# The norm in mid-layer in two halves of the tokens

## The chip, the core and the metric

The kernel runs on one core of a Trainium2 chip. The metric is the device time in microseconds of one execution; lower is better. A core has five engines that run side by side, each in its own order, and meet at semaphores: TensorE (PE, matmuls, with the weight loads shown apart as PEld), VectorE (DVE), ScalarE (ACT), GpSimd (POOL) and SyncE (SP). The last two issue DMAs here.

## What is computed

A trunk of two layers over 512 tokens of width 1024, all in float32. Each layer has two residual steps:

```python
h = modulate(rms_norm(x, norm1_g[l]), sh1, sc1)
z = h @ w_in[l]
# conformer convolution, short gated convolution and differential attention on parts of z
x = x + g1[:, None, :] * mix          # mix = concat(ya, yb, yc) @ w_out[l]
h = modulate(rms_norm(x, norm2_g[l]), sh2, sc2)
x = x + g2[:, None, :] * swiglu(h, w_gate_up[l], w_down[l])
# rms_norm(x, g) = x * rsqrt(mean(x * x, -1) + 1e-6) * g
# modulate(h, shift, scale) = h * (1 + scale) + shift
```

The second norm of a layer, between the projection `w_out` and the gate/up product, is the one that the change touches. It is a norm over the 1024 features of each token, so the tokens are independent of each other.

## The kernel before

**Layout.** Features lie on partitions, tokens in columns: `xT` is 128 partitions x 8 chunks x 512 tokens. Each product is made from two parts of either side: `h_hi` and `h_lo`, `w_hi` and `w_lo` (FP32R), with three matmuls per 128x128 block (hi x hi, lo x hi, hi x lo; `product`, L1308). TensorE writes a result of 128 features x 512 tokens into one of the eight PSUM banks.

**Units.** The weights come as a stream of units of 128x1024, in the order in which TensorE uses them. A unit is loaded by SP into one of two `raw` buffers, ScalarE copies it to `w_hi` (`split_hi`, L547), and VectorE subtracts to get `w_lo` (`split_lo`, L852). For units 12 to 33 of layer 0 (`lo_by_dma`, L60) ScalarE writes the negative copy as well, and POOL issues a DMA that adds the raw weights to it (`add_raw`, L435). Four units fit in the ring, so unit u + 4 is split when unit u is done: that is `step(u)` (L554) on ScalarE. SP's next load into a raw buffer waits for the split of the unit in it. A unit is 8 blocks, 24 matmuls (`unit`, L1323).

**The projection.** Eight units, U_OUT to U_OUT+7, give the eight chunks of `mix`. After each, VectorE adds it to `xT` (`add_to_x`, L1100), ScalarE squares the new chunk (`square_x`, L560), VectorE sums the squares (`norm_sum`, L1091). Chunk 7's square is not summed by VectorE.

**The norm.** `norm_stat` (L1384, called in L1573) makes two FP32 matmuls with a matrix of ones, of the sum of seven squares and of the square of chunk 7; each is two instructions in the profile. ScalarE takes Ln and Exp of that (`norm_rstd`, L568, called in L821); ahead of it, in ScalarE's order, stands `step(U + U_OUT + 7)` (L820), which splits unit U_GU+3. Then the eight chunks of h are made: VectorE scales a chunk by gain and rstd into one of two buffers (`norm_apply`, L927), ScalarE adds the shift and writes `h_hi` (`norm_hi`, L584), VectorE writes `h_lo` (`norm_lo`, L936). VectorE's order is scaling 0, scaling 1, difference 0, scaling 2, difference 1 and so on (`norm`, L944); a scaling from the third on waits until the difference two chunks before, the instruction ahead of it, has ended.

**Gate/up.** The first two units, U_GU and U_GU+1, go chunk by chunk into banks 0 and 1, as the chunks of h arrive (`units_by_chunk`, L1331, called in L1575): four matmuls per chunk after `h_hi`, two more after `h_lo`. The third and the fourth unit follow whole, and then the other 40 in a loop.

All orders are written out by hand; there is no scheduler. ScalarE's around the norm:

```python
for s in range(N_OUT):
    if s < N_OUT - 1:
        step(U + U_OUT + s)
    square_x(2 * l + 1, s)
step(U + U_OUT + N_OUT - 1)
norm_rstd(2 * l + 1)
```

## Time and profile before

| | us |
|---|---|
| runs (3): median, lowest, highest | 1224.09, 1223.81, 1224.74 |
| the profiled execution | 1223.83 |
| its span in the profile | 1222.0 |
| TensorE busy in the span | 1185.0 (97%) |
| VectorE busy | 709.3 (58%) |
| ScalarE busy | 487.2 (40%) |
| mean granted clock of TensorE | 0.989 of full |

The span is the time from the first to the last instruction of one execution, the device time is a little longer. A busy time is the time in which at least one instruction of the engine was in flight. Matmuls are pipelined, so one of 0.39 us is followed by the next after less than that; their spacing is read from the starts. "[idle before <-releaser]" behind an instruction is the time that its engine stood still before it, and what ended that. The granted clock is a share of TensorE's full clock of 2.4 GHz; its other level, 0.50, is 1.2 GHz.

### The profile page before, as it was taken

The numbers are of one execution on the slowest core, as the hardware profiler recorded it, in microseconds if no ns is written. First come the engines' busy times: TensorE is split into PE (matmuls) and PEld (weight loads), VectorE is DVE, ScalarE is ACT, GpSimd is POOL, SyncE is SP. The second block draws the span as 40 slices with busy tenths as digits, with TensorE's granted clock in tenths as the row PEclk, the third lists the DMA queues.
The fourth block names the chain that finished last, engine by engine and source line by source line (L and its number), as shares of the span: only waits on it lengthen the run. The fifth ranks groups of instructions, "written<-read, shape, count | busy, mean of one in ns | idle before, by whom it ended". The sixth has DMA issues, their size and how long they took to land.

```text
span 1222.0 us, 14230 instructions
## 1 busy us (share of the span) xinstructions
PE 1185.0 (97%) x5102; PEld 928.4 (76%) x5102; DVE 709.3 (58%) x1014; ACT 487.2 (40%) x728; POOL 111.7 (9%) x185
## 2 busy tenths in 40 slices
PE   8999999789999999999989999999999999999998
PEld 6887545668888888888868875467788888888887
DVE  7888987766556433466656999746633333333331
ACT  5556787552322322322242356774432232322220
POOL 2411322211012000111000001000000000000000
PEclk9999999889999999999989999999999999999999
DMA  8787455976565222677413321103223223233322
GB/s 306 249 232 161 95 111 203 297 207 224 189 198 185 97 103 88 261 253 246 148 56 104 100 71 52 52 1 121 78 94 103 86 103 102 87 103 104 104 103 86
DMA packets 47498, 169.92 MB, mean 139 GB/s; under 512 B 5537, under 2 KB 5665, under 8 KB 47458
## 3 DMA queue, kind: packets, MB, share of 16 engines
q1 hardware_dynamic: 30386, 107.13, 25.9%
q0 software_dynamic: 17072, 62.27, 17.1%
q8 instruction: 23, 0.38, 0.1%
q14 instruction: 17, 0.14, 0.0%
HBM read 167.28 MB, written 2.10 MB: 139 GB/s over the span
## 4 chain that ended last, share of the span: by engine, by line
PE 80%; DVE 11%; ACT 5%; issue 3%; DMA 1%; POOL 0%; DVEq 0%; ACTq 0%
PE ps L1311 22%; PE ps L1313 21%; PE ps L1312 21%; PE ps L1341 3%; DVE uc L974 3%; ACT prob L632 2%; PE ps L1525 1%; PE ps L1345 1%; DVE w_lo L857 1%; PE ps L1357 1%; PE ps L1358 1%; PE ps L1362 1%; DVE neg_max L1055 1%; PE ps L1372 1%; PE ps L1374 1%
## 5 line engine op out<-in xcount | busy, mean ns | idle before, releaser
L550 ACT ACTIVATE w_hi<-raw 128x1024 fp32r<-128x1024 f32 x196 | 207.7, 1060 | 574.6 <-PE ps L1313 492.9
L857 DVE TENSOR_TENSOR w_lo<-raw,w_hi 128x1024 fp32r<-128x1024 f32 x174 | 213.4, 1227 | 266.5 <-ACT w_hi L550 266.3
L1311 PE MATMUL ps<-h_hi,w_hi 128*128 128x512 f32 x848 | 335.9, 396 | 7.0 <-DMA w_lo<-w_stream 7.0
L1313 PE MATMUL ps<-h_lo,w_hi 128*128 128x512 f32 x848 | 331.3, 391 | 0.0
L1312 PE MATMUL ps<-h_hi,w_lo 128*128 128x512 f32 x848 | 331.2, 391 | 0.0
L1311 PEld LDWEIGHTS ps<-h_hi,w_hi 128*128 128x128 f32 x848 | 159.9, 189 | 56.0 <-issue 16.7
L1313 PEld LDWEIGHTS ps<-h_lo,w_hi 128*128 128x128 f32 x848 | 159.8, 188 | 33.9
L1312 PEld LDWEIGHTS ps<-h_hi,w_lo 128*128 128x128 f32 x848 | 160.0, 189 | 31.7
L1311 PE MATMUL ps<-gu_hi,w_hi 128*128 128x512 f32 x352 | 136.9, 389 | 0.0
L1312 PE MATMUL ps<-gu_hi,w_lo 128*128 128x512 f32 x352 | 136.9, 389 | 0.0
L1313 PE MATMUL ps<-gu_lo,w_hi 128*128 128x512 f32 x352 | 136.9, 389 | 0.0
L1259 DVE TENSOR_TENSOR work_b<-ps,work_a 128x512 f32<-128x512 f32 x44 | 30.4, 692 | 115.5 <-PE ps L1313 92.1
L974 DVE SCALAR_TENSOR_TENSOR uc<-ua,pcol,uc 128x512 f32<-128x512 f32 x120 | 83.6, 743 | 0.0
L1312 PEld LDWEIGHTS ps<-gu_hi,w_lo 128*128 128x128 f32 x352 | 66.1, 188 | 13.8
L1311 PEld LDWEIGHTS ps<-gu_hi,w_hi 128*128 128x128 f32 x352 | 66.1, 188 | 13.7
L1313 PEld LDWEIGHTS ps<-gu_lo,w_hi 128*128 128x128 f32 x352 | 66.1, 188 | 13.7
L1372 PE MATMUL ps<-w_hi,h_hi 128*128 128x512 f32 x192 | 75.0, 391 | 1.1 <-DVE w_lo L857 1.1
L1374 PE MATMUL ps<-w_hi,h_lo 128*128 128x512 f32 x192 | 74.7, 389 | 0.0
L1373 PE MATMUL ps<-w_lo,h_hi 128*128 128x512 f32 x192 | 74.7, 389 | 0.0
L632 ACT ACTIVATE prob<-ps,neg_max 128x512 f32<-128x512 f32 x64 | 43.3, 683 | 33.6 <-DVE neg_max L1055 33.6
L1104 DVE SCALAR_TENSOR_TENSOR xT<-ps,mod,xT 128x512 f32<-128x512 f32 x32 | 24.0, 750 | 56.1 <-PE ps L1313 53.6
L444 POOL TENSOR_SCALAR row_mix<-row_inv,neg_lam 128x1 f32<-128x1 f32 x32 | 25.7, 803 | 219.7 <-DVE row_inv L1062 219.7
(171 smaller groups left out, 1312.8 us busy)
## 6 DMA issues: line engine op xcount, KB each, us to landing
raw<-w_stream SPq DMA_DIRECT2D x196, 512.0 KB, 3.3
ada_ring_gu<-ada POOLq DMA_DIRECT2D x28, 512.0 KB, 4.2
ada_ring_late<-ada POOLq DMA_DIRECT2D x28, 512.0 KB, 4.9
w_lo<-w_stream POOLq DMA_DIRECT2D x22, 512.0 KB, 8.1
ada_ring_first<-ada POOLq DMA_DIRECT2D x16, 512.0 KB, 5.7
ada_ring_mid_a<-ada POOLq DMA_DIRECT2D x12, 512.0 KB, 5.5
ada_ring_mid_b<-ada POOLq DMA_DIRECT2D x12, 512.0 KB, 5.4
xT<-x_t SPq DMA_DIRECT2D x4, 512.0 KB, 5.7
```

The source lines that it names most:

```text
L550: act.activation(w_hi[:, u % RING, :], raw[:, u % RAW, :], ACT.Copy).then_inc(s_whi, 1)
L632: act.activation(prob[:, it % PROBS, comp, :], ps[:, 2 * (it % 2) + comp, :], ACT.Exp, bias=neg_max[:, it, comp:comp + 1], accum_out=row_s ...
L857: dve.tensor_tensor(w_lo[:, u % RING, :], raw[:, u % RAW, :], w_hi[:, u % RING, :].bitcast(F32), ALU.subtract).then_inc(s_wlo, 1)
L974: dve.scalar_tensor_tensor(uc[:, c, :], ua[:, c, j:j + T], w, uc[:, c, :], ALU.mult, ALU.add).then_inc(s_tap, 1)
L1259: dve.tensor_tensor(wb[:, f, :], ps[:, j, :], wa[:, f, :], ALU.mult).then_inc(s_pr, 1)
L1311: pe.matmul(dst, whi, rhs[0][:, n, :], start=start, stop=False)
L1312: pe.matmul(dst, wlo, rhs[0][:, n, :], start=False, stop=False)
L1313: return pe.matmul(dst, whi, rhs[1][:, n, :], start=False, stop=stop)
L1341: pe.matmul(ps[:, bank, :], wp[:, u % RING, n * P:(n + 1) * P], h_hi[:, n, :], start=b == 0 and wp is w_hi, stop=False)
L1372: pe.matmul(ps[:, bank, :], hs[0], ws[0], start=n == 0, stop=False)
L1373: pe.matmul(ps[:, bank, :], hs[0], ws[1], start=False, stop=False)
L1374: return pe.matmul(ps[:, bank, :], hs[1], ws[0], start=False, stop=n == KC - 1)
```

## The change

In each layer the stretch from the last projection unit to the first two gate/up units is done in two halves of the tokens, columns 0 to 255 and 256 to 511:

- The last unit writes its first half into bank 6 and its second into bank 2, one after the other, in 48 matmuls of 256 columns. Amid the second half (after four blocks) the statistic of the first half is taken.
- VectorE adds each half to chunk 7 of `xT`, ScalarE squares it. In layer 0 the second gain (`make_gain`) is made ahead of these additions instead of after.
- Ln and Exp are taken of each half; those of the second half stand in ScalarE's order behind `h_hi` of chunk 2 of the first half.
- VectorE goes through the eight chunks for the first half, then for the second.
- TensorE's first two gate/up units go through the eight chunks for the first half, then for the second, with the second half's statistic after two chunks of the first. A chunk's six matmuls wait for `h_lo`, so for both parts.
- The split of unit U_GU+3 moves: on ScalarE from ahead of the norm's Ln to between the two halves of `h_hi`, in layer 1 on VectorE from ahead of the scaling to behind chunk 1 of the second half.

The diff, without the new semaphores and blank lines:

```diff
+HALVES = (slice(0, T // 2), slice(T // 2, T))
...
+        B_LAST, B_HALF_STAT = (6, 2), (7, 4)
...
+            def square_half(l, half):
+                act.wait_ge(s_xnew if half else s_xhalf, KC * (2 * l + 1) if half else l + 1)
+                act.wait_ge(s_sum, (KC - 1) * 2 * l + KC - 2)
+                c = HALVES[half]
+                act.activation(wa[:, 1, c], xT[:, KC - 1, c], ACT.Square).then_inc(s_sq if half else s_sqhalf, 1)
+            def rstd_half(l, half):
+                n = 2 * l + 1
+                c = HALVES[half]
+                if half:
+                    act.wait_ge(s_nstat, n + 1)
+                    act.activation(rstd[:, 0, c], ps[:, B_HALF_STAT[half], c], ACT.Ln, scale=1.0 / D,
+                                   bias=eps[:]).then_inc(s_nln, 1)
+                    act.wait_ge(s_nln, n + 1)
+                    act.activation(rstd[:, 0, c], rstd[:, 0, c], ACT.Exp, scale=-0.5).then_inc(s_nrs, 1)
+                else:
+                    act.wait_ge(s_sthalf, l + 1)
+                    act.activation(rstd[:, 0, c], ps[:, B_HALF_STAT[half], c], ACT.Ln, scale=1.0 / D,
+                                   bias=eps[:]).then_inc(s_lnhalf, 1)
+                    act.wait_ge(s_lnhalf, l + 1)
+                    act.activation(rstd[:, 0, c], rstd[:, 0, c], ACT.Exp, scale=-0.5).then_inc(s_rshalf, 1)
+            def hi_half(l, half, k):
+                n = 2 * l + 1
+                c = HALVES[half]
+                if half:
+                    act.wait_ge(s_t, KC * n + k + 1)
+                else:
+                    act.wait_ge(s_thalf, KC * l + k + 1)
+                a = mod_at(SH2, k)
+                act.activation(h_hi[:, k, c], wb[:, k % 2, c], ACT.Identity,
+                               bias=mod[:, l, a:a + 1]).then_inc(s_hhi if half else s_hihalf, 1)
...
                 for s in range(N_OUT):
                     if s < N_OUT - 1:
                         step(U + U_OUT + s)
-                    square_x(2 * l + 1, s)
-                step(U + U_OUT + N_OUT - 1)
-                norm_rstd(2 * l + 1)
+                        square_x(2 * l + 1, s)
+                square_half(l, 0)
+                rstd_half(l, 0)
+                square_half(l, 1)
                 act.wait_ge(s_gain, 2 * l + 1)
                 for k in range(KC):
-                    norm_hi(l, 1, k)
+                    hi_half(l, 0, k)
+                    if k == 2:
+                        rstd_half(l, 1)
+                step(U + U_OUT + N_OUT - 1)
+                for k in range(KC):
...
+            def norm_halves(l):
+                n = 2 * l + 1
+                dve.wait_ge(s_gain, n)
+                for half in range(2):
+                    c = HALVES[half]
+                    if half:
+                        dve.wait_ge(s_nrs, n + 1)
+                    else:
+                        dve.wait_ge(s_rshalf, l + 1)
+                    for k in range(KC + 1):
+                        if k < KC:
+                            if k >= 2 and half:
+                                dve.wait_ge(s_h, KC * n + k - 1)
+                            elif k >= 2:
+                                dve.wait_ge(s_hhalf, KC * l + k - 1)
+                            dve.scalar_tensor_tensor(wb[:, k % 2, c], xT[:, k, c], gain[:, l, 1, k:k + 1],
+                                                     rstd[:, 0, c], ALU.mult,
+                                                     ALU.mult).then_inc(s_t if half else s_thalf, 1)
+                        if k:
+                            a = mod_at(SH2, k - 1)
+                            if half:
+                                dve.wait_ge(s_hhi, KC * n + k)
+                            else:
+                                dve.wait_ge(s_hihalf, KC * l + k)
+                            dve.scalar_tensor_tensor(h_lo[:, k - 1, c], wb[:, (k - 1) % 2, c], mod[:, l, a:a + 1],
+                                                     h_hi[:, k - 1, c].bitcast(F32), ALU.add,
+                                                     ALU.subtract).then_inc(s_h if half else s_hhalf, 1)
+                        if half and k == 2:
+                            split_lo(UNITS * l + U_GU + RING - 1)
...
+            def add_last_to_x(l, unit):
+                a = mod_at(G1, KC - 1)
+                for half in range(2):
+                    c = HALVES[half]
+                    if half:
+                        dve.wait_ge(s_unit, unit)
+                    else:
+                        dve.wait_ge(s_uhalf, l + 1)
+                    dve.scalar_tensor_tensor(xT[:, KC - 1, c], ps[:, B_LAST[half], c], mod[:, l, a:a + 1],
+                                             xT[:, KC - 1, c], ALU.mult,
+                                             ALU.add).then_inc(s_xnew if half else s_xhalf, 1)
...
-                    add_to_x(l, s, B_OUT[s], G1, U + U_OUT + s + 1)
-                    split_lo(U + U_OUT + s + RING)
+                    if s < N_OUT - 1:
+                        add_to_x(l, s, B_OUT[s], G1, U + U_OUT + s + 1)
+                    else:
+                        if l == 0:
+                            make_gain(0, 1)
+                        add_last_to_x(l, U + U_OUT + s + 1)
+                    if s < N_OUT - 1:
+                        split_lo(U + U_OUT + s + RING)
                     if s < N_OUT - 1:
                         norm_sum(2 * l + 1, s)
                     if l == 0 and s < N_OUT - 2:
                         for m in range(M_MID + 12 + 2 * s - (s == 0), M_MID + 14 + 2 * s):
                             mod_dot(m)
-                if l == 0:
-                    make_gain(0, 1)
-                norm(l, 1)
+                norm_halves(l)
...
+            def stat_half(l, half):
+                n = 2 * l + 1
+                c = HALVES[half]
+                pe.wait_ge(s_sum, (KC - 1) * n)
+                pe.matmul(ps[:, B_HALF_STAT[half], c], ones[:], sq_sum[:, c], start=True, stop=False)
+                if half:
+                    pe.wait_ge(s_sq, KC * (n + 1))
+                else:
+                    pe.wait_ge(s_sqhalf, l + 1)
+                pe.matmul(ps[:, B_HALF_STAT[half], c], ones[:], wa[:, 1, c], start=False,
+                          stop=True).then_inc(s_nstat if half else s_sthalf, 1)
+            def product_half(bank, w, b, half, start, stop):
+                c = HALVES[half]
+                whi, wlo = w_hi[:, w, b * P:(b + 1) * P], w_lo[:, w, b * P:(b + 1) * P]
+                pe.matmul(ps[:, bank, c], whi, h_hi[:, b, c], start=start, stop=False)
+                pe.matmul(ps[:, bank, c], wlo, h_hi[:, b, c], start=False, stop=False)
+                return pe.matmul(ps[:, bank, c], whi, h_lo[:, b, c], start=False, stop=stop)
+            def last_unit(l, u):
+                weights_split(u)
+                for half in range(2):
+                    if half:
+                        pe.wait_ge(s_xnew, 2 * KC * l + 4)
+                    for b in range(KC):
+                        if half and b == KC // 2:
+                            stat_half(l, 0)
+                        mm = product_half(B_LAST[half], u % RING, b, half, b == 0, b == KC - 1)
+                    mm.then_inc(s_unit if half else s_uhalf, 1)
+            def first_units(l, us):
+                n = 2 * l + 1
+                for u in us:
+                    weights_split(u)
+                for half in range(2):
+                    for b in range(KC):
+                        if half:
+                            pe.wait_ge(s_h, KC * n + b + 1)
+                        else:
+                            pe.wait_ge(s_hhalf, KC * l + b + 1)
+                        for bank, u in enumerate(us):
+                            mm = product_half(bank, u % RING, b, half, b == 0, b == KC - 1)
+                            if half and b == KC - 1:
+                                mm.then_inc(s_unit, 1)
+                        if not half and b == 1:
+                            stat_half(l, 1)
...
-                    unit(U + U_OUT + s, B_OUT[s], h, order)
-                norm_stat(2 * l + 1)
-
-                units_by_chunk([U + U_GU, U + U_GU + 1], (0, 1), order, s_hhi, s_h, KC * (2 * l + 1))
+                    if s < N_OUT - 1:
+                        unit(U + U_OUT + s, B_OUT[s], h, order)
+                    else:
+                        last_unit(l, U + U_OUT + s)
+                first_units(l, [U + U_GU, U + U_GU + 1])
```

## Rows read from the trace of the kernel before

**Rows 1.** The page: busy time by engine; the chain that ended last, by engine
```profile
PE 1185.0 (97%) x5102; PEld 928.4 (76%) x5102; DVE 709.3 (58%) x1014; ACT 487.2 (40%) x728; POOL 111.7 (9%) x185
...
PE 80%; DVE 11%; ACT 5%; issue 3%; DMA 1%; POOL 0%; DVEq 0%; ACTq 0%
```

**Rows 2.** TensorE's timeline, layer 0: start us, us, engine, line, operation, count, [idle before]
```profile
252.70 1.02 PE L1387 MATMUL ps<-sq_sum,ones 128*128 128x512 f32 x2
...
254.45 1.12 PE L1389 MATMUL ps<-work_a,ones 128*128 128x512 f32 x2 [0.73 <-ACT work_a L566]
...
259.27 0.76 PE L1341 MATMUL ps<-h_hi,w_hi 128*128 128x512 f32 x1 [3.69 <-ACT h_hi L588]
...
272.70 0.39 PE L1311 MATMUL ps<-h_hi,w_hi 128*128 128x512 f32 x1
...
278.14 0.39 PE L1311 MATMUL ps<-h_hi,w_hi 128*128 128x512 f32 x1
```

**Rows 3.** TensorE's timeline, layer 1
```profile
851.91 1.02 PE L1387 MATMUL ps<-sq_sum,ones 128*128 128x512 f32 x2
...
857.83 0.47 PE L1341 MATMUL ps<-h_hi,w_hi 128*128 128x512 f32 x1 [3.13 <-ACT h_hi L588]
...
870.47 0.39 PE L1311 MATMUL ps<-h_hi,w_hi 128*128 128x512 f32 x1
```

**Rows 4.** Stretches: length, busy us of PE, PEld, DVE, ACT, POOL, granted clock, DMA, GB/s
```profile
257.00:259.00 2.00, 0.00 (x0) 0.00 (x0) 1.42 (x2) 1.12 (x2) 0.47 (x1) 0.65 1.04 225
264.00:265.00 1.00, 1.00 (x5) 0.75 (x5) 0.96 (x3) 0.35 (x1) 0.00 (x0) 0.78 0.09 16
858.00:859.00 1.00, 1.00 (x4) 0.82 (x4) 0.96 (x2) 0.30 (x1) 0.00 (x0) 0.68 0.58 234
```

**Rows 5.** VectorE's timeline, layer 0
```profile
250.63 0.15 DVE L916 TENSOR_TENSOR mod<-mod_raw,pcol 128x3 f32<-128x3 f32 x1
...
257.55 1.42 DVE L933 SCALAR_TENSOR_TENSOR work_b<-xT,gain,rstd 128x512 f32<-128x512 f32 x2 [3.75 <-ACT rstd L572]
...
259.16 0.75 DVE L941 SCALAR_TENSOR_TENSOR h_lo<-work_b,mod,h_hi 128x512 fp32r<-128x512 f32 x1 [0.19 <-ACT h_hi L588]
...
259.94 0.75 DVE L933 SCALAR_TENSOR_TENSOR work_b<-xT,gain,rstd 128x512 f32<-128x512 f32 x1
...
260.61 0.75 DVE L941 SCALAR_TENSOR_TENSOR h_lo<-work_b,mod,h_hi 128x512 fp32r<-128x512 f32 x1
```

**Rows 6.** ScalarE's timeline, layer 0
```profile
255.25 1.04 ACT L552 ACTIVATE w_lo<-raw 128x1024 fp32r<-128x1024 f32 x1
...
256.19 0.67 ACT L570 ACTIVATE rstd<-ps,eps 128x512 f32<-128x512 f32 x1
...
256.89 0.63 ACT L572 ACTIVATE rstd<-rstd 128x512 f32<-128x512 f32 x1
...
260.73 0.72 ACT L588 ACTIVATE h_hi<-work_b,mod 128x512 fp32r<-128x512 f32 x1 [0.99 <-DVE work_b L933]
```

**Rows 7.** Groups of VectorE and ScalarE by form: count, busy us, mean ns, idle before
```profile
L857 DVE TENSOR_TENSOR w_lo<-raw,w_hi 128x1024 fp32r<-128x1024 f32 x174 | 213.4, 1227 | 266.5 <-ACT w_hi L550 266.3
...
L1046 DVE TENSOR_TENSOR tb<-tn,tabs 128x256 f32<-128x256 f32 x32 | 12.1, 418 | 0.0
...
L1041 DVE TENSOR_TENSOR ta<-tn,tabs 128x512 f32<-128x512 f32 x16 | 11.1, 692 | 0.6
...
L550 ACT ACTIVATE w_hi<-raw 128x1024 fp32r<-128x1024 f32 x196 | 207.7, 1060 | 574.6 <-PE ps L1313 492.9 <-PE ps L1374 49.3 <-DMA raw<-w_stream 15.1
...
L566 ACT ACTIVATE work_a<-xT 128x512 f32<-128x512 f32 x24 | 14.9, 620 | 18.6 <-DVE xT L1104 18.5
```

**Rows 8.** TensorE's timeline, keys' transposes in layer 0
```profile
105.26 1.91 PE L1458 MATMUL ps<-ident,qk 128*128 128x128 f32 x16
```

**Rows 9.** The page's DMA issues: count, KB each, median us to landing
```profile
raw<-w_stream SPq DMA_DIRECT2D x196, 512.0 KB, 3.3
...
w_lo<-w_stream POOLq DMA_DIRECT2D x22, 512.0 KB, 8.1
```

More of the change, by code:

```diff
@@ L325, in encoder_kernel @@
         s_h = sem("h_ready")
+        s_uhalf = sem("first_half_unit_done")
+        s_xhalf = sem("first_half_x_updated")
+        s_sqhalf = sem("first_half_x_squared")
+        s_sthalf = sem("first_half_norm_stat")
+        s_lnhalf = sem("first_half_norm_ln")
+        s_rshalf = sem("first_half_norm_rstd")
+        s_thalf = sem("first_half_norm_scaled")
+        s_hihalf = sem("first_half_h_hi_ready")
+        s_hhalf = sem("first_half_h_ready")
         s_sig = sem("gate_sigmoid")
@@ L818, in _ @@
                         step(U + U_OUT + s)
-                    square_x(2 * l + 1, s)
-                step(U + U_OUT + N_OUT - 1)
-                norm_rstd(2 * l + 1)
+                        square_x(2 * l + 1, s)
+                square_half(l, 0)
+                rstd_half(l, 0)
+                square_half(l, 1)
                 act.wait_ge(s_gain, 2 * l + 1)
                 for k in range(KC):
-                    norm_hi(l, 1, k)
+                    hi_half(l, 0, k)
[3 more added lines that the diff above has]
+                for k in range(KC):
+                    hi_half(l, 1, k)
                 act.preload_act_table_set("silu_and_others")
```

## Prediction

> **What bounds the kernel now.** I read the chain of waits first: TensorE carries 80% of what ends last [rows 1], so only a stretch where TensorE stands still, or runs slowly, can pay. The norm in mid-layer is one, once in each of the two layers. TensorE's timeline shows it. In layer 0 the last unit of the projection has been issued at 252.70 us and the third gate/up unit starts at 272.70: 20.00 us for two sums of squares and two units [rows 2]. In layer 1 it is 851.91 to 870.47, 18.56 us [rows 3]. A unit is 24 matmuls in 278.14 - 272.70 = 5.44 us, 0.227 each [rows 2], so two cost 10.88; the rest, 9.1 and 7.7 us, is the norm. In it TensorE's work is four FP32 instructions of some 0.43, 1.7 us. What is left is waiting (TensorE stands 3.69 us in layer 0 and 3.13 in layer 1 before the first gate/up matmul [rows 2, 3]) and a lower clock. The stretches show the granted clock at 0.65 in 257 to 259 us, on its way from the 2.4 to the 1.2 GHz level after TensorE had been idle since 255.6; it is back within 264 to 265, and in layer 1 it falls in 858 to 859 [rows 4].
>
> The last view is VectorE's. Once the statistic is there, a chunk of h costs a scaling (L933) and a difference (L941): 0.67 from scaling to difference, 0.78 back, where VectorE waits for its own difference to have ended [rows 5]. That is 1.45 us per chunk, against 6 x 0.227 = 1.36 for TensorE. So the two are nearly even, and the change must be priced on both.
>
> **The change, step by step.** Times from here on count from the first matmul of the last unit, 5.44 us before the stretch above: 247.26 us in layer 0, 846.47 in layer 1. In the kernel before, the third gate/up unit starts at 25.44 (layer 0) and 24.00 (layer 1). All stages behind it move with it, as TensorE has no other long wait in a layer's second half; so its new start is the whole effect.
>
> *Prices of a half.* A VectorE operation on 256 columns takes 418 ns, on 512 692 [rows 7]: 0.274 less. The scaling and the difference take 0.75 and follow each other by 0.67 [rows 5]; halves: 0.48 and 0.40, or 0.52 where the next waits for the end. A half chunk is then 0.92, two 1.84 instead of 1.45. ScalarE: 1060 ns for 1024 columns, 620 for 512 [rows 7], so 0.22 less: h_hi 0.50, square 0.40, Ln 0.46, Exp 0.41 [rows 6]. TensorE on 256 columns with these weights is not in the trace. From below it is half of 0.227, 0.113; at 2.4 GHz 512 columns are 0.213, which leaves 0.013 fixed and gives 0.107 + 0.013 = 0.120; from above it is the weight load's own 0.18 (928.4 us in 5102 [rows 1]), if that no longer hides. I take 0.120, because sixteen FP32 transposes of 128 columns, each with its own load, pass in 1.91 us, 0.12 each at most [rows 8], so a load needs no more.
>
> *Last unit.* First half 24 x 0.120 = 2.88; its sum can be added at 3.1, but VectorE is still with the sixth square, mod and gain (250.63 plus two short operations, 3.7 here [rows 5]). Addition and square of chunk 7 end at 4.7. TensorE meanwhile has done four blocks of the second half (4.32) and the first FP32 sum (4.75); so the make_gain moved ahead (0.15) is hidden. The statistic ends at 5.2, the second half at 6.6. Ln and Exp are ready at 6.3, hidden by the second addition, for which VectorE waits until 6.8. The first scaling starts at 7.2 against 257.55 - 247.26 = 10.29 before [rows 5]: **3.1 us earlier**. h_hi and h_lo follow, TensorE begins at 8.9 instead of 12.0 (layer 1: 11.4).
>
> *First half of h.* VectorE delivers a half chunk every 0.92 us, TensorE uses 6 x 0.120 = 0.72. After two chunks (10.5) comes the other half's statistic, 0.85, to 11.4. On ScalarE Ln and Exp of it stand behind h_hi of chunk 2 and ahead of h_hi of chunk 3, and ScalarE is in order: it waits from 9.9 to 11.6, spends 0.9, and h_hi of chunk 3, which could have begun at 10.4, begins at 12.4. Behind it wait VectorE's h_lo, then TensorE. **A new stall of 1.9 us**: h_lo of chunk 3 ends at 13.4, of chunk 7 at 16.9; TensorE ends the half at 17.7.
>
> *Second half of h, layer 0.* ScalarE has first to do the moved split of unit U_GU+3: two copies of 0.94 each [rows 6]. Its h_hi starts at 18.1, h_lo of chunk 0 ends at 19.2, of chunk 7 at 19.2 + 6 x 0.92 + 0.7 = 25.4. TensorE's last block ends at 26.2. **Layer 0: 26.2 - 25.4 = 0.8 us later.** The split's add-DMA waits on POOL for the negative copy: some 18.1, plus 8.1 to land [rows 9], is 26.2, and U_GU+3 is wanted at 26.2 + 5.4 = 31.7, so a unit covers it. SP's next raw load waits for the same copy and needs 3.3 [rows 9], landing long before ScalarE takes it after 26. Without that cover each microsecond late would be one of TensorE's. Behind POOL's add stand loads that wait for products of the gate/up stage, later anyway.
>
> *Layer 1.* One copy on ScalarE, so h_lo of chunk 0 ends at 18.3; but VectorE does the moved w_lo behind chunk 1, 1.14 (1227 ns, less 0.08 of overlap) [rows 7]. Chunk 7 ends at 25.5, TensorE at 26.4. **Layer 1: 26.4 - 24.0 = 2.4 us later.**
>
> *Sum:* +0.8 + 2.4 = +3.2 us. The 3 us gained at the start go to 16 half chunks at 0.92 where 8 whole ones cost 1.45 (3.1 us per layer), and the two stalls come on top; what TensorE got back from the lower clock was never on VectorE's path. The 72 additional matmuls per layer (0.013 each, 0.9) lie mostly in TensorE's new waits. With 0.113 per half matmul, and 0.02 less for each hand-over, the sum is +2.1; with 0.125 and 0.03 more, +4.5. Against the profiled execution, 1223.83 (span 1222.0; 0.26 below the median of the runs, 1224.09), that is 1227.0. About 0.2%, 2.4 us, is what a measurement of this kernel can tell from no change.
>
> A rule on the waits: before, VectorE's next scaling starts 0.78 after a difference whose end it waits for, and a difference starts 0.67 after a scaling whose end it doesn't [rows 5], so that wait costs 0.11. The Trainium skill's page "VectorE: DVE Perf Modes", section "The DRAIN you can't avoid", says that a semaphore between chained operations costs nothing extra. By the row the sum is +3.2; by the rule each half chunk would be 0.81 and the sum +1.1. The row decides.
>
> **Rivals.** *A, not slower:* the fixed part of VectorE's halves does not come twice, and the half scaling and difference follow by 0.335. Then a half chunk is 0.74, TensorE's 0.72 keeps step, and the layers come out at -1.5 and +0.1: 1222.5. For it: no scalar_tensor_tensor of 256 columns is in the trace, and the first scaling does start 3 us earlier. Against: 418 ns and not 346 for the two-tensor form [rows 7]. It decides from about 0.35 us downwards; with both stalls gone too it would be about 1220.
>
> *B, the clock falls in the new gaps:* TensorE stands from 6.6 to 8.9, 12.1 to 13.5 and 17.7 to 19.3 (18.4 in layer 1), and works 0.72 of every 0.92 between. Before, it fell some 2 us into the gap of layer 0 [rows 2, 4], so 2.3 could be enough. At 1.2 GHz a chunk's six half matmuls take up to 1.44, more than 0.92, and the statistic 1.7. A fall at 9 to 10 costs some 1.6 per layer, one late in the second half up to 2.4: 1228.6 in one layer, 1230.2 in both. Against: in layer 1 the whole gap of 3.13 us passed at the full clock, which fell only in 858 to 859 [rows 3, 4].
>
> *C, half matmuls bound by the weight load:* at 0.18 each a chunk takes 1.09, and the layers come out at +6.1 and +7.4: 1237.3. Against: [rows 8], and 0.227 for 512 columns, which leaves no room for a load in series. The Trainium skill, "TensorE: Matmul & The Clock Gate", section "Measured speedup vs the span model", has a load overlap only matmuls of other rows of the array; that would put loads in series here. By that rule C's price or more would hold; the trace disagrees, with 0.227 per pair.
>
> **Chances.** Forecast 0.50, A 0.20, B 0.22, C 0.08. Of the forecast 0.15 falls within 0.2% (+2.1 to +2.4, and what the steps leave uncertain), of A 0.12, the rest of A is faster; B and C are slower. So faster 0.08, same 0.27, slower 0.65. The range leaves out C, A's lower end and B's upper: 1223.0 to 1231.0.
>
> **What the next profile would show.** First scaling 3 us earlier after the last unit began; a step of about 0.92 between half chunks; an idle ScalarE of 1.7 us ahead of the second Ln; h_hi of chunk 3 some 2 us behind chunk 2's successor on VectorE; TensorE's waits split into many of 0.2 us and three of 1.4 to 2.3; the third gate/up unit 26 us behind the last unit's start in both layers. A step of 0.8 or less, or a missing ScalarE stall, would make the prediction wrong to the fast side; half matmuls 0.15 or more apart, or a granted clock of 0.5 in the stretch, to the slow side.

## The result, and the profile after

The kernel with the change took 1228.57 us (median of 6 runs, 1227.85 to 1230.05), the kernel before 1224.74 beside it (6 runs): a ratio of 1.0034, 95% interval 1.0022 to 1.0045. It is slower by some 4 us. The profiled execution of after took 1228.17 us (span 1226.4), that of before 1223.83 (span 1222.0): 4.4 us more in the span.

The page's busy times and the chain of waits, to be held against [rows 1]:

```profile
PE 1188.1 (97%) x5254; PEld 936.0 (76%) x5254; DVE 715.4 (58%) x1048; ACT 493.0 (40%) x750; POOL 112.7 (9%) x185
...
PE 78%; DVE 11%; ACT 5%; issue 3%; DMA 2%; SPq 0%; POOL 0%; DVEq 0%; ACTq 0%
```

VectorE and ScalarE are 6 us busier each, with 34 and 22 instructions more, which is the fixed part of their halves; on the page alone nothing else can be told. The time shows in TensorE's timeline. The first row of each layer below is the first matmul of the last unit, the last one the third gate/up unit [rows 2, 3]:

```profile
248.34 0.28 PE L1512 MATMUL ps<-h_hi,w_hi 128*128 128x256 f32 x1
248.45 0.28 PE L1513 MATMUL ps<-h_hi,w_lo 128*128 128x256 f32 x1
...
257.41 0.36 PE L1512 MATMUL ps<-h_hi,w_hi 128*128 128x256 f32 x1 [2.18 <-DVE h_lo L1035]
...
259.35 1.05 PE L1500 MATMUL ps<-sq_sum,ones 128*128 128x256 f32 x2
...
268.90 0.39 PE L1512 MATMUL ps<-h_hi,w_hi 128*128 128x256 f32 x1 [1.28 <-DVE h_lo L1035]
...
275.94 0.40 PE L1415 MATMUL ps<-h_hi,w_hi 128*128 128x512 f32 x1
...
848.26 0.28 PE L1512 MATMUL ps<-h_hi,w_hi 128*128 128x256 f32 x1
...
857.22 0.35 PE L1512 MATMUL ps<-h_hi,w_hi 128*128 128x256 f32 x1 [2.18 <-DVE h_lo L1035]
...
858.85 0.59 PE L1500 MATMUL ps<-sq_sum,ones 128*128 128x256 f32 x2
...
861.81 0.39 PE L1512 MATMUL ps<-h_hi,w_hi 128*128 128x256 f32 x1 [1.22 <-DVE h_lo L1035]
...
874.73 0.40 PE L1415 MATMUL ps<-h_hi,w_hi 128*128 128x512 f32 x1
```

From the last unit's start to the third gate/up unit ("the stretch" from here on) it is 275.94 - 248.34 = 27.60 us in layer 0, where before had 25.44, and 874.73 - 848.26 = 26.47 in layer 1, where before had 24.00: +2.16 and +2.47, together +4.63. The rest of the span adds up to -0.2: the part ahead of layer 0's stretch is 1.08 longer (248.34 against 247.26), the part between the two stretches 1.45 shorter (572.32 against 573.77), the end 0.14 longer.

One thing differs between the layers. In layer 1 the two matmuls on sq_sum take 0.59 us, in layer 0 1.05. The table of stretches (columns as in [rows 4]) shows why:

```profile
256.00:258.00 2.00, 0.59 (x5) 0.62 (x6) 1.73 (x5) 1.29 (x4) 0.00 (x0) 1.00 1.07 385
258.00:260.00 2.00, 2.00 (x11) 1.83 (x11) 1.54 (x4) 0.32 (x1) 0.00 (x0) 0.66 1.03 227
260.00:262.00 2.00, 2.00 (x8) 1.73 (x8) 0.00 (x0) 0.68 (x2) 0.00 (x0) 0.50 0.41 84
...
858.00:860.00 2.00, 2.00 (x15) 1.86 (x14) 1.37 (x3) 0.22 (x2) 0.00 (x0) 1.00 0.00 0
```

In layer 0 the granted clock, full in 256 to 258, is 0.66 in 258 to 260 and 0.50 in 260 to 262, the 1.2 GHz level, after TensorE had stood 2.18 us and done a few matmuls. In layer 1 the same wait of 2.18 us passed without it.

ScalarE's timeline, around the second half's Ln (L595), answers to [rows 6]:

```profile
261.29 0.47 ACT L595 ACTIVATE rstd<-ps,eps 128x256 f32<-128x256 f32 x1 [2.97 <-PE ps L1505]
...
859.92 0.47 ACT L595 ACTIVATE rstd<-ps,eps 128x256 f32<-128x256 f32 x1 [1.78 <-PE ps L1505]
```

VectorE's timeline answers to [rows 5]: the first scalings, the pace of the half chunks, and VectorE's waits for h_hi of chunk 3 (262.65 and 861.27) and of the second half's first chunk behind the moved split (268.36):

```profile
255.66 0.87 DVE L1026 SCALAR_TENSOR_TENSOR work_b<-xT,gain,rstd 128x256 f32<-128x256 f32 x2
...
257.29 0.48 DVE L1026 SCALAR_TENSOR_TENSOR work_b<-xT,gain,rstd 128x256 f32<-128x256 f32 x1
257.69 0.48 DVE L1035 SCALAR_TENSOR_TENSOR h_lo<-work_b,mod,h_hi 128x256 fp32r<-128x256 f32 x1
258.21 0.48 DVE L1026 SCALAR_TENSOR_TENSOR work_b<-xT,gain,rstd 128x256 f32<-128x256 f32 x1
...
262.65 0.48 DVE L1035 SCALAR_TENSOR_TENSOR h_lo<-work_b,mod,h_hi 128x256 fp32r<-128x256 f32 x1 [3.03 <-ACT h_hi L615]
...
268.36 0.48 DVE L1035 SCALAR_TENSOR_TENSOR h_lo<-work_b,mod,h_hi 128x256 fp32r<-128x256 f32 x1 [1.02 <-ACT h_hi L615]
...
861.27 0.48 DVE L1035 SCALAR_TENSOR_TENSOR h_lo<-work_b,mod,h_hi 128x256 fp32r<-128x256 f32 x1 [1.85 <-ACT h_hi L615]
```

The first scaling came 7.32 us after the last unit's start (255.66 - 248.34), 3 us sooner than before's 10.29. From there on it is given back.

### The profile page after: what moved, and what is told of

Its sections match the earlier page's. It is cut to its first block, busy times and chain, and to the rows that moved or that the text cites. A ratio compares the mean times of both kernels' runs of the same rounds, so it can differ in the third digit from the quotient of the medians.

```text
span 1226.4 us, 14591 instructions
## 1 busy us (share of the span) xinstructions
PE 1188.1 (97%) x5254; PEld 936.0 (76%) x5254; DVE 715.4 (58%) x1048; ACT 493.0 (40%) x750; POOL 112.7 (9%) x185
## 4 chain that ended last, share of the span: by engine, by line
PE 78%; DVE 11%; ACT 5%; issue 3%; DMA 2%; SPq 0%; POOL 0%; DVEq 0%; ACTq 0%
PE ps L1415 21%; PE ps L1417 21%; PE ps L1416 21%; DVE uc L1061 3%; ACT prob L682 2%; PE ps L1681 1%; DVE w_lo L913 1%; PE ps L1445 1%; PE ps L1461 1%; DVE neg_max L1142 1%; PE ps L1462 1%; PE ps L1656 1%; PE ps L1466 1%; PE ps L1476 1%; PE ps L1477 1%
## 5 line engine op out<-in xcount | busy, mean ns | idle before, releaser
L1415 PE MATMUL ps<-h_hi,w_hi 128*128 128x512 f32 x832 | 329.6, 396 | 7.1 <-DMA w_lo<-w_stream 7.1
L1417 PE MATMUL ps<-h_lo,w_hi 128*128 128x512 f32 x832 | 325.1, 391 | 0.0
L1416 PE MATMUL ps<-h_hi,w_lo 128*128 128x512 f32 x832 | 325.0, 391 | 0.0
L1415 PEld LDWEIGHTS ps<-h_hi,w_hi 128*128 128x128 f32 x832 | 156.9, 189 | 55.4 <-issue 16.7
L1417 PEld LDWEIGHTS ps<-h_lo,w_hi 128*128 128x128 f32 x832 | 156.7, 188 | 33.1
L1416 PEld LDWEIGHTS ps<-h_hi,w_lo 128*128 128x128 f32 x832 | 157.0, 189 | 31.2
```

The source lines that it names most:

```text
L1415: pe.matmul(dst, whi, rhs[0][:, n, :], start=start, stop=False)
L1416: pe.matmul(dst, wlo, rhs[0][:, n, :], start=False, stop=False)
L1417: return pe.matmul(dst, whi, rhs[1][:, n, :], start=False, stop=stop)
```

## The experiments

Because the parts outside the two stretches vary by one or two microseconds from profile to profile, each experiment is read first by its two stretches (layer 0 / layer 1; before 25.44 / 24.00, after 27.60 / 26.47). Where a few microseconds of the whole had to be told, it was also timed against the kernel before. The diffs are against the kernel with the change, unless another is named.

### e1: the second half's statistic ahead of the first half's products

```diff
@@ first_units @@
+                stat_half(l, 1)
                 for half in range(2):
...
-                        if not half and b == 1:
-                            stat_half(l, 1)
```

> TensorE takes the second half's statistic right after the last unit, where it stands for 2.2 us, instead of behind two chunks of the first half. The stretch counted is from the first matmul of the last unit to the third gate/up unit: 25.44 us (layer 0) and 24.00 (layer 1) before, 27.60 and 26.47 with the change. Theory 1 (VectorE's chain of half chunks and the waits in ScalarE's order set the end): ScalarE's wait ahead of the second Ln (2.97 and 1.78 us) goes, the 0.9 us of Ln and Exp stay, some 0.4 of it on the chain: 24.5 and 24.8, so 1223.7 to 1225 in all. Theory 2 (the granted clock is what costs): layer 1, where the clock stayed full with the change, remains at 26.5. Theory 3 (the 72 additional matmuls per layer cost): both layers unchanged but for the clock.

Measured: 24.41 / 24.58. The single execution took 1221.52 us beside 1223.91 for before, which is more than the stretches explain (-0.45 in all) and within what the rest varies by. ScalarE's timeline of layer 0 has no wait left ahead of the second Ln:

```profile
256.84 0.45 ACT L595 ACTIVATE rstd<-ps,eps 128x256 f32<-128x256 f32 x1
```

Without ScalarE's wait the stretch is 3.2 us shorter in layer 0 and 1.9 in layer 1. TensorE's longest wait ahead of the gate/up products also fell, from 2.18 to 0.59 us, so this run alone doesn't tell the clock from the wait; e3 does.

### e2: the moved split inside ScalarE's wait

```diff
@@ ScalarE @@
                     if k == 2:
+                        step(U + U_OUT + N_OUT - 1)
                         rstd_half(l, 1)
-                step(U + U_OUT + N_OUT - 1)
@@ norm_halves @@
+                        if not half and k == 4:
+                            split_lo(UNITS * l + U_GU + RING - 1)
...
-                        if half and k == 2:
-                            split_lo(UNITS * l + U_GU + RING - 1)
```

> Only the split of unit U_GU+3 moves: on ScalarE ahead of the second Ln, into its wait of 2.97 and 1.78 us, in layer 1 on VectorE into its wait ahead of the difference of chunk 3, first half. Theory 1: the second half of h no longer begins late: VectorE's waits of 1.02 us (layer 0) and the 1.14 us of w_lo (layer 1) go, 26.5 in layer 0 with the same clock and 25.4 in layer 1; 1226.0 to 1226.5 in all. Theories 2 and 3: 27.6 and 26.5 remain.

Measured: 26.90 / 25.47, a single execution of 1228.01 us. ScalarE now does the two copies first and still waits:

```profile
259.64 1.04 ACT L564 ACTIVATE w_hi<-raw 128x1024 fp32r<-128x1024 f32 x1
260.59 1.04 ACT L566 ACTIVATE w_lo<-raw 128x1024 fp32r<-128x1024 f32 x1
...
262.96 0.47 ACT L595 ACTIVATE rstd<-ps,eps 128x256 f32<-128x256 f32 x1 [1.33 <-PE ps L1505]
```

In layer 1, where the clock stayed, the split that stood in the path was worth 1.0 us. Layer 0 got only 0.7: the clock fell there too (0.50 in 260 to 262), and the second Ln came 262.96 - 249.86 = 13.10 us after the last unit's start, where the change has 12.95.

### e3: matmuls in TensorE's three long gaps

Nine, five and three matmuls of ones on ones, 128 columns wide, are added into a PSUM bank that is free then. Their result isn't used; all else is as in the change.

```diff
+            def warm_half(n):
+                for _ in range(n):
+                    pe.matmul(ps[:, 3, 0:P], ones[:], ones[:], start=True, stop=True)
@@ first_units @@
+                pe.wait_ge(s_xnew, 2 * KC * l + 5)
...
+                            if b == 0:
+                                warm_half(3)
                             pe.wait_ge(s_h, KC * n + b + 1)
                         else:
+                            if b in (0, 3):
+                                warm_half(9 if b == 0 else 5)
```

> Matmuls of a 128x128 matrix of ones into a bank that nobody reads then (9, 5 and 3 of them, some 0.21 us each) fill TensorE's three long gaps; nothing else changes. Theory 2: with the clock full throughout, both layers come back to 25.4 and 24.0 or less. Theory 1: only layer 0 gains, about 1.2 us, because there the statistic on ScalarE's path ran at the lower clock: 26.2 to 26.6; layer 1 stays at 26.4 to 26.7. Theory 3: no change beyond the clock, as the additional matmuls are still there.

Measured: 26.30 / 26.48, a single execution of 1227.18 us. The granted clock is 1.00 from 256 to 264, and ScalarE's wait in layer 0 is back at what layer 1 shows without any addition. The ends of layer 0's stretch, a row of the clock, and the second Ln:

```profile
247.95 0.28 PE L1512 MATMUL ps<-h_hi,w_hi 128*128 128x256 f32 x1
...
274.25 0.40 PE L1415 MATMUL ps<-h_hi,w_hi 128*128 128x512 f32 x1
```

```profile
258.00:260.00 2.00, 2.00 (x15) 1.89 (x15) 1.08 (x3) 0.39 (x1) 0.00 (x0) 1.00 1.08 236
```

```profile
259.61 0.48 ACT L595 ACTIVATE rstd<-ps,eps 128x256 f32<-128x256 f32 x1 [1.79 <-PE ps L1505]
```

So in layer 0 the lower clock made 27.60 of 26.30: 1.3 us. In layer 1 it made nothing. Against e3, e1 is 1.89 faster in layer 0 and 1.90 in layer 1: that is ScalarE's wait by itself, at the same clock.

### e7: products of h_hi ahead of the wait for h_lo

Each half chunk waits for its h_hi only (s_hhi, in the first half s_hihalf), does the four products on it, then waits for h_lo and does the other two.

```diff
@@ first_units, each half chunk @@
+                            pe.wait_ge(s_hhi, KC * n + b + 1)
...
+                        for bank, u in enumerate(us):
+                            for wp in (w_hi, w_lo):
+                                pe.matmul(ps[:, bank, c], wp[:, u % RING, b * P:(b + 1) * P], h_hi[:, b, c],
+                                          start=b == 0 and wp is w_hi, stop=False)
...
-                            mm = product_half(bank, u % RING, b, half, b == 0, b == KC - 1)
+                            mm = pe.matmul(ps[:, bank, c], w_hi[:, u % RING, b * P:(b + 1) * P], h_lo[:, b, c],
+                                           start=False, stop=b == KC - 1)
```

> The change as it is, but a half chunk's four products of h_hi are taken when h_hi is there, and only the two of h_lo wait for h_lo, as in the kernel before. Theory 1: the last four of six matmuls leave the end of the chain, 0.5 us, and the second statistic comes 0.4 earlier: 26.3 to 26.8 in layer 0 (with the lower clock; 25.4 without) and 25.6 in layer 1, against 27.60 and 26.47. If TensorE's own time bound the stretch, nothing would change.

Measured: 26.41 / 25.51, a single execution of 1226.67 us, as expected. TensorE starts after 1.66 us instead of 2.18 and ScalarE's wait is 2.37 / 1.31 us instead of 2.97 / 1.78: an earlier start of the products moves the statistic behind them forward by 0.6 and 0.5 us. The rest of the gain lies at the end, where four of the last chunk's six products are done before its h_lo is there. Layer 1's last difference and third gate/up unit in this run, then the last difference of the change:

```profile
872.30 0.48 DVE L1035 SCALAR_TENSOR_TENSOR h_lo<-work_b,mod,h_hi 128x256 fp32r<-128x256 f32 x1 [0.18 <-ACT h_hi L615]
...
873.23 0.40 PE L1415 MATMUL ps<-h_hi,w_hi 128*128 128x512 f32 x1
```

```profile
873.32 0.48 DVE L1035 SCALAR_TENSOR_TENSOR h_lo<-work_b,mod,h_hi 128x256 fp32r<-128x256 f32 x1 [0.18 <-ACT h_hi L615]
```

That is 873.23 - 872.30 = 0.93 us against 874.73 - 873.32 = 1.41, so the order of the products costs the change 0.48 us there, and as much in layer 0. The runs e1, e2, e3 and e6 have this order too; the kernel before, e4, e5, e8 and e9 have the other.

### e6: both waits removed, all chunks still in halves

This is e1, and VectorE's moved split behind the whole norm.

```diff
-                        if half and k == 2:
-                            split_lo(UNITS * l + U_GU + RING - 1)
...
                 norm_halves(l)
+                split_lo(U + U_GU + RING - 1)
```

> All eight chunks in halves as with the change, the second statistic right after the last unit, and layer 1's w_lo of the moved split behind the last chunk on VectorE: the waits that ScalarE's and VectorE's orders put into the chain are away, the price of sixteen half chunks stays. Theory 1: 24.5 in layer 0 (VectorE still waits 1 us for h_hi behind the split's two copies) and 23.7 in layer 1, together 1.2 us ahead of the kernel before: 1222.8, no difference that can be told.

Measured: 24.41 / 23.58; 1221.90 us (median of 12 runs), ratio 0.9984, interval 0.9974 to 0.9995. Layer 1 gained 1.00 from e1, the price of the split on VectorE's path. With both waits gone the halves come out 1.45 us ahead of before by the stretches (47.99 against 49.44), where 1.2 were expected and held to be too little to tell. Besides the halves two things are left in it: the order of the products (e7), and in layer 0 VectorE's wait for h_hi behind the split's two copies. That wait is 0.18 us in layer 1 (at 860.43), and the 0.83 between them is what layer 0 is longer by:

```profile
263.32 0.48 DVE L1035 SCALAR_TENSOR_TENSOR h_lo<-work_b,mod,h_hi 128x256 fp32r<-128x256 f32 x1 [1.01 <-ACT h_hi L615]
```

### e5: only the statistic in halves, h in whole chunks

```diff
@@ ScalarE @@
+                rstd_half(l, 1)
                 for k in range(KC):
-                    hi_half(l, 0, k)
-                    if k == 2:
-                        rstd_half(l, 1)
...
+                    norm_hi(l, 1, k)
+                    if k == 3:
+                        step(U + U_OUT + N_OUT - 1)
@@ VectorE @@
-                norm_halves(l)
+                dve.wait_ge(s_rshalf, l + 1)
+                norm(l, 1)
+                split_lo(U + U_GU + RING - 1)
@@ TensorE @@
-                first_units(l, [U + U_GU, U + U_GU + 1])
+                stat_half(l, 1)
+                units_by_chunk([U + U_GU, U + U_GU + 1], (0, 1), order, s_hhi, s_h, KC * (2 * l + 1))
```

> Halves only up to the statistic: the last unit, the additions to chunk 7, the squares, both statistics (the second right after the last unit), Ln and Exp; the eight chunks of h and the first two gate/up units are done whole, as before the change. The split stands behind h_hi of chunk 3 on ScalarE and behind the last chunk on VectorE. Theory 1: VectorE begins 9.9 us after the last unit's first matmul, only 0.4 ahead of the kernel before, but pays 8 x 1.45 for h, and TensorE, which no longer stands for 3 us and more, runs at the full clock: third gate/up unit at 23.4 (layer 0) and 22.8 (layer 1), together 3.3 us ahead of the kernel before, 1220.6. If an early start of h is what counts, it is no faster than 24.5 in layer 0 and 23.5 in layer 1, 1223.

Measured: 23.74 / 23.85; 1223.32 us (median of 12 runs), ratio 0.9994, interval 0.9983 to 1.0004. Layer 1 missed by 1.0. I had reckoned with the full clock; the stretches of layer 0, then layer 1, show another:

```profile
258.00:260.00 2.00, 1.29 (x3) 1.13 (x4) 1.84 (x3) 1.23 (x2) 0.00 (x0) 0.63 0.97 203
260.00:262.00 2.00, 2.00 (x6) 1.52 (x6) 1.97 (x4) 1.10 (x2) 0.00 (x0) 0.52 0.09 16
...
856.00:858.00 2.00, 2.00 (x6) 1.61 (x5) 1.93 (x4) 0.87 (x2) 0.00 (x0) 0.50 0.03 8
```

TensorE had stood 2.76 us in both layers before that.

### e8: e5 with that gap filled

Eleven matmuls of ones on ones, whose result isn't used (`warm_half` as in e3), stand ahead of the gate/up products. The diff is against e5.

```diff
                 stat_half(l, 1)
+                pe.wait_ge(s_xnew, 2 * KC * l + 5)
+                warm_half(11)
                 units_by_chunk([U + U_GU, U + U_GU + 1], (0, 1), order, s_hhi, s_h, KC * (2 * l + 1))
```

> This is the kernel with whole chunks of h behind the halved statistic, and in TensorE's wait of 2.76 us ahead of the first gate/up matmul 11 matmuls of ones on ones (128 columns, two passes of 0.12 us each, 2.66 us in all) whose result isn't used. There the stretch from the first matmul of the last unit to the third gate/up unit was 23.74 (layer 0) and 23.85 (layer 1), with the first gate/up matmuls up to 0.43 us apart. Theory (the lower clock after that wait took the missing gain): the pace is 0.227 per matmul from the start, limited by VectorE's 1.45 us a chunk, and the stretch is 22.7 to 23.3 in both layers; against the kernel before (25.44 and 24.00) some -3.3 us, a ratio near 0.997. Rival (VectorE's and ScalarE's order sets the pace, the clock hides behind it): 23.6 to 24.0 in both, ratio 0.999. If the additional matmuls end late they add up to 0.3 us.

Measured: 23.10 / 22.59; 1218.55 us (median of 8 runs), ratio 0.9962, interval 0.9950 to 0.9975. TensorE's timeline in layer 0, and the clock where e5 had 0.63 and 0.52:

```profile
255.00 2.62 PE L1532 MATMUL ps<-ones 128*128 128x128 f32 x22
257.93 0.47 PE L1445 MATMUL ps<-h_hi,w_hi 128*128 128x512 f32 x1 [0.31 <-ACT h_hi L638]
```

```profile
258.00:260.00 2.00, 2.00 (x9) 1.65 (x10) 1.97 (x3) 1.06 (x2) 0.00 (x0) 1.00 0.76 154
260.00:262.00 2.00, 2.00 (x11) 1.60 (x10) 1.93 (x4) 1.27 (x3) 0.00 (x0) 1.00 0.02 4
```

The lower clock had cost e5 0.64 us in layer 0 and 1.26 in layer 1, more than it had missed by (0.34 and 1.05).

### e9: the kernel before, with its gap filled

The change is not in this one. In the kernel before TensorE's timeline has no wait between the first gate/up product and the third unit of [rows 2, 3], so it must have been behind VectorE there, and the lower clock of [rows 4] may have been on the path after all. Twelve matmuls of ones on ones, whose result isn't used, go into the wait; the diff is against the kernel before.

```diff
                 norm_stat(2 * l + 1)
+                pe.wait_ge(s_xnew, 2 * KC * l + 5)
+                for _ in range(12):
+                    pe.matmul(ps[:, 3, 0:P], ones[:], ones[:], start=True, stop=True)
```

> This is the kernel before, unchanged but for 12 matmuls of ones on ones (128 columns, 0.24 us each in two passes, 2.9 us in all) in TensorE's wait of 3.69 us (layer 0) and 3.13 us (layer 1) behind the statistic; their result isn't used. In the kernel before TensorE ran without a wait from the first gate/up matmul to the third unit in both layers, so it was behind VectorE: the last difference ended some 269.5 and 868.1 us, the third unit started at 272.70 and 870.47. Theory (the lower clock behind that wait set the end of the stretch before, and not VectorE's 1.45 us a chunk as my prediction had it): at the full clock TensorE follows VectorE, last difference plus two matmuls of 0.227, so the stretch is 22.7 (layer 0) and 22.0 (layer 1) instead of 25.44 and 24.00, 4.7 us less in all, a ratio near 0.996. Rival (my prediction's statement, what TensorE gets back from the clock is not on VectorE's path): 25.0 or more and 23.6 or more, no difference that can be told. If the additional matmuls alone don't keep the clock up, the stretch stays as it was.

Measured: 23.35 / 22.71, that is 2.09 and 1.29 less; 1220.26 us (median of 6 runs), ratio 0.9966, interval 0.9953 to 0.9979. TensorE, from the last unit's first matmul on, and the stretches, layer 0:

```profile
250.88 0.39 PE L1311 MATMUL ps<-h_hi,w_hi 128*128 128x512 f32 x1
...
259.03 2.84 PE L1576 MATMUL ps<-ones 128*128 128x128 f32 x24
262.89 0.47 PE L1341 MATMUL ps<-h_hi,w_hi 128*128 128x512 f32 x1 [1.02 <-ACT h_hi L588]
...
274.23 0.39 PE L1311 MATMUL ps<-h_hi,w_hi 128*128 128x512 f32 x1
```

```profile
262.00:264.00 2.00, 1.11 (x5) 0.96 (x6) 1.78 (x3) 1.33 (x2) 0.00 (x0) 1.00 1.03 266
264.00:266.00 2.00, 2.00 (x11) 1.63 (x10) 1.97 (x4) 0.92 (x2) 0.00 (x0) 1.00 1.08 262
```

The first scaling is where it was (261.18 - 250.88 = 10.30), and TensorE's start too; only the pace behind it changed. The expectation was 0.7 us too low in both layers, because I counted two products behind the last difference and not the six that each chunk needs from its h_hi on (h_hi of chunk 7 ends at 272.34, its first product starts at 272.86, behind those of chunk 6, and the third unit at 274.23).

### e4: only the first three chunks in halves

Chunks 0 to 2 are done in halves, 3 to 7 whole; the second statistic stands ahead of the products, both splits go where nothing waits for them, and TensorE takes h_hi's products ahead of h_lo's.

```diff
+M = 3
@@ ScalarE @@
-                for k in range(KC):
+                for k in range(M):
                     hi_half(l, 0, k)
-                    if k == 2:
+                    if k == 1:
                         rstd_half(l, 1)
-                step(U + U_OUT + N_OUT - 1)
...
+                for k in range(M, KC):
+                    norm_hi(l, 1, k)
+                    if k == M + 1:
+                        step(U + U_OUT + N_OUT - 1)
@@ norm_halves @@
+                seq = [(half, k) for half in range(2) for k in range(M)] + [(2, k) for k in range(M, KC)]
+                cols = HALVES + (slice(0, T),)
...
+                for i in range(len(seq) + 1):
+                    if i < len(seq):
+                        scale(*seq[i])
+                    if i:
+                        low(*seq[i - 1])
+                split_lo(UNITS * l + U_GU + RING - 1)
@@ first_units @@
+                stat_half(l, 1)
...
+                for half, b in [(half, b) for half in range(2) for b in range(M)] + [(2, b) for b in range(M, KC)]:
```

> The early start is kept and most of its price taken away: only chunks 0 to 2 are done in halves, chunks 3 to 7 whole; the second statistic comes right after the last unit, its Ln and Exp behind h_hi of chunk 1; the split stands behind h_hi of chunk 4 on ScalarE and behind the last chunk on VectorE; TensorE takes the products of h_hi ahead of h_lo again. Theory 1: VectorE's chain is 6 x 0.92 + 5 x 1.45 = 12.8 us from 7.2 on instead of 14.7 plus the waits: the third gate/up unit at 22.1 (layer 0) and 21.5 (layer 1), 3.4 and 2.5 us ahead of the kernel before, so 1218.4 (0.995). Theory 3: as 48 + 36 half matmuls per layer remain, the gain against the change would be under 1 us. Theory 2: the gain would be that of the clock alone, in layer 0, and the result not below the kernel before.

Measured: 21.79 / 21.22; 1218.01 us (median of 6 runs, 1215.32 to 1219.14), ratio 0.9946, interval 0.9934 to 0.9958. It is faster than both kernels, by the same early start that the change has. The granted clock is 1.00 in all of 254 to 266 and of 854 to 864, with no filling, since TensorE never stands longer than 0.59 us there. VectorE's timeline holds another reading:

```profile
258.97 0.48 DVE L1044 SCALAR_TENSOR_TENSOR h_lo<-work_b,mod,h_hi 128x256 fp32r<-128x256 f32 x1
259.37 0.48 DVE L1033 SCALAR_TENSOR_TENSOR work_b<-xT,gain,rstd 128x256 f32<-128x256 f32 x1
...
260.56 0.48 DVE L1044 SCALAR_TENSOR_TENSOR h_lo<-work_b,mod,h_hi 128x256 fp32r<-128x256 f32 x1
261.07 0.48 DVE L1033 SCALAR_TENSOR_TENSOR work_b<-xT,gain,rstd 128x256 f32<-128x256 f32 x1
```

At 258.97 the next scaling doesn't wait for the end of the difference just ahead of it, and follows after 0.40; at 260.56 it does, and follows after 0.51. Same operations, same kernel: that wait costs 0.11 us.

## Why the prediction was right, and where it was not

Side and range held: slower, 1228.57 in 1223.0 to 1231.0, forecast 1227.0. That the total came so near is in part luck: the steps added up to +3.2, at most +4.5 by their own margins, and the two stretches measured +4.63, while the medians are only 3.83 apart, as the rest of a run varies. By its steps:

- **The early start** was right: first scaling at 7.32 and 7.21 us (855.47 - 848.26), forecast 7.2.
- **Prices of a half** were right: half matmuls 0.12 apart, scaling and difference 0.40 and 0.52 apart, 0.92 for a half chunk. This takes rival A and rival C out. The Trainium skill, "TensorE: Matmul & The Clock Gate", section "The mechanism" (the prediction names the section behind it), lets a load overlap only matmuls of other rows of the array; the trace disagrees, as each of these half matmuls has a load of its own, 0.19 us over all 128 rows, and they still follow each other after 0.12 us.
- **The hand-over on VectorE** was right at 0.11 to 0.12 (after's 0.52 against 0.40; e4). The Trainium skill, "VectorE: DVE Perf Modes", section "The DRAIN you can't avoid", measured on chained copies that a semaphore costs nothing extra; for these operations the trace disagrees, with 0.51 against 0.40 in one kernel (e4).
- **ScalarE's stall** of 1.9 us on h_hi of chunk 3 was right in kind and, at the full clock, in size: e3 less e1 is 1.89 and 1.90. I forecast 1.7 us idle ahead of the second Ln; layer 1 had 1.78.
- **The split in layer 1** was right: forecast 1.14 on VectorE, and removing it gave 1.00 (e1 to e6).
- **Layer 1's term** was right: forecast 26.4 and +2.4, measured 26.47 and +2.47.
- **Layer 0's term** is the step that failed: "Layer 0: 26.2 - 25.4 = 0.8 us later", measured +2.16. At the full clock it would have held (e3: 26.30). Rival B, to which I gave 0.22 and 1.6 us a layer for an early fall, came true in layer 0 and not in layer 1. The clock was 0.66 and 0.50 from 258 to 262, so the second statistic, which starts at 259.35, ran at half speed, as did the products just ahead of it, and ScalarE behind it waited 2.97 us instead of 1.79. That is 1.2 of the 1.3 us that e3 gives back.
- **A sentence beside the sum was wrong**: "what TensorE got back from the lower clock was never on VectorE's path". In the kernel before it was on the path, for 2.09 and 1.29 us (e9). The sum was not touched, since it starts from before's measured 25.44 and 24.00, but the picture was. With both kernels at the full clock, e3 against e9, the change costs 26.30 - 23.35 = 2.95 and 26.48 - 22.71 = 3.77, 6.7 us; in the kernels as they are 2.1 of that does not show, because before loses 3.4 to the clock and after 1.3.

So the account, at the full clock throughout, against e9's 46.06 for both layers: the change 52.78 (e3). ScalarE's wait takes 3.8 of it (e3 to e1), VectorE's split in layer 1 1.0 (e1 to e6). What stays is 1.9 (e6, 47.99), and not all of it is the price of the halves: some 1.0 is the order of the products (0.48 a layer by e7, and e9 has the other order), 0.8 the wait behind the split in layer 0 (e6). Without these two the sum would be about e9's, by an estimate that no run tried. Eight chunks in halves, 8 x 0.39 = 3.1 us a layer, use up what the early start gives, 3.0 us in layer 0 and 2.4 in layer 1 (7.21 against 9.65). Three chunks in halves (e4) bring the sum to 43.01, 3.05 below e9, which has the same order of the products; of the 4.98 below e6 some 1.0 should be that order, which was not tried by itself in e4.

The halved statistic by itself, with the moved split, brings little at the full clock: e8 against e9 is 0.25 in layer 0 and 0.12 in layer 1.

## What to carry to other kernels

Halve only as much of a pipeline as it takes to bridge the wait at its start: each half that comes after pays the fixed part again, here 0.39 us a chunk on VectorE. When work is interleaved on in-order engines, look at what stands behind the instruction that waits for the other half; here one reduction issued two chunks late cost 1.9 us in each layer. And where a tensor engine runs without a gap behind a long wait, look at its granted clock before taking another engine's pace for the bound: twelve matmuls whose result isn't used were alone worth 0.34% here (e9).

## What the runs showed of the hardware that I had not expected

The same wait is not always followed by the same clock. After 2.18 us without work the clock fell in layer 0 of the change and stayed in layer 1 of the same execution. e2 and e7 show the same after 2.19 and 1.66 us: 0.50 in 260 to 262 (e2) and 0.54 in 258 to 260 (e7), both in layer 0, and 1.00 in the whole stretch of layer 1. What sets layer 0 apart the runs don't show. After 2.76 us (e5) and 3.13 and 3.69 us (before) it fell each time, in layer 0 by the time the work came back, in layer 1 some 0.2 us (e5: 0.92 in 855 to 856, work from 855.62) and 0.5 us (before) after it.

The norm at the start of layer 1, which both kernels compute with the same operations, shows it too. These are stretches of before, where TensorE's work came back at 627.13 after 3.47 us:

```profile
627.00:630.00 3.00, 2.87 (x7) 2.33 (x8) 2.92 (x5) 1.32 (x2) 0.00 (x0) 0.50 0.20 78
630.00:633.00 3.00, 3.00 (x9) 2.32 (x8) 2.93 (x6) 1.50 (x3) 0.00 (x0) 0.50 0.00 0
```

and of after, where it came back at 630.09 after 3.17 us:

```profile
630.00:631.00 1.00, 0.91 (x4) 0.76 (x5) 0.96 (x2) 0.56 (x1) 0.00 (x0) 0.85 0.64 250
631.00:634.00 3.00, 3.00 (x9) 2.35 (x8) 2.93 (x5) 1.44 (x2) 0.00 (x0) 0.50 0.00 0
```

Before spent some 5.9 us of work at the 1.2 GHz level there, after some 3.4 (the clock was at 0.96 in 633 to 634 of before, and at 0.94 in 634 to 635 of after). At half speed that is 1.3 us, about the 1.45 that the part between the stretches is shorter; it was not tried by itself. It is one reason why a single execution could not tell 2 us here (e1), and the stretches of its profile could.
